# Each slot of the high and low weights 64 bytes longer than its chunk, and the low parts of x and h 32 bytes further on

## The reference

```python
for layer in range(DEPTH_2):
    g = norm_gains[layer]
    h = x + 0.5 * swiglu(rmsnorm_2(x, g[0]), w_ffn_gu[layer, 0], w_ffn_down[layer, 0])
    xn = rmsnorm_2(h, g[1])
    ...
    h = h + mix
    h = h + 0.5 * swiglu(rmsnorm_2(h, g[2]), w_ffn_gu[layer, 1], w_ffn_down[layer, 1])
    gate = jax.nn.sigmoid(rmsnorm_2(h, g[3]) @ w_ple_gate[layer])
    x = h + gate * (p[layer] @ w_ple_proj[layer])
```

## The kernel before

| distance in a partition, bytes | before |
|---|---|
| from `w_hi` to `w_lo`, same slot | 24960 |
| from one slot to the next | 4096 |
| from `w_lo` slot 0 to `xn_hi` | 24768 |
| from `xn_hi` to `xn_lo` | 16384 |
| from `xn_lo` to `h_hi`, then to `h_lo` | 16384, 4096 |

## Time and profile before

### The profile page before, as it was taken

The page is one execution under the profiler, slowest core; times in us unless marked ns, Lnnn a source line. Parts: engine busy times, 40 slices in busy tenths (PEclk is TensorE's granted clock), DMA queues, the critical chain, the costliest instruction groups (busy, mean ns, idle before and its releaser), DMA issues.

```text
span 2417.1 us, 51817 instructions
## 1 busy us (share of the span) xinstructions
PE 2405.2 (100%) x20462; PEld 2376.4 (98%) x20462; DVE 1725.2 (71%) x2425; ACT 1317.1 (54%) x2019; POOL 90.2 (4%) x91
## 2 busy tenths in 40 slices
PE   9999999999999999999999999999999999999999
PEld 9999999999999999999999999999999999999999
DVE  8878867558776677667766776688667766877666
ACT  5756655447564464445544554467445544766444
POOL 1000000001100000000000000000000000220000
PEclk9999999999999999999999999999999999999999
DMA  7325326555355556555466565643655656535653
GB/s 268 115 65 172 123 80 221 185 185 166 123 189 189 197 167 212 189 182 188 135 202 197 171 204 192 194 137 132 204 189 182 200 193 190 165 125 189 194 195 125
DMA packets 115378, 418.86 MB, mean 173 GB/s; under 512 B 12832, under 2 KB 14112, under 8 KB 114976
## 3 DMA queue, kind: packets, MB, share of 16 engines
q1 hardware_dynamic: 114096, 412.40, 52.2%
q0 software_dynamic: 560, 2.10, 0.3%
q10 hardware_dynamic: 576, 2.27, 0.2%
HBM read 414.62 MB, written 2.10 MB: 172 GB/s over the span
## 4 chain that ended last, share of the span: by engine, by line
PE 94%; DVE 3%; ACT 2%; DMA 1%; issue 0%; ACTq 0%; SPq 0%; DVEq 0%
PE ps_gu L140 17%; PE ps_gu L146 17%; PE ps_gu L141 17%; PE ps_acc L140 8%; PE ps_acc L146 8%; PE ps_acc L141 8%; PE ps_acc L2739 1%; PE ps_acc L2297 1%; DVE w_lo L100 1%; PE ps_misc L140 1%; PE ps_gu L2333 1%; PE ps_misc L141 1%; PE ps_misc L146 1%; PE ps_sum L140 1%; PE ps_sum L146 1%; PE ps_sum L141 1%
## 5 line engine op out<-in xcount | busy, mean ns | idle before, releaser
L100 DVE TENSOR_TENSOR w_lo<-w_raw,w_hi 128x1024 fp32r<-128x1024 f32 x781 | 953.0, 1228 | 378.8 <-ACT w_hi L92 370.3
L140 PE MATMUL ps_gu<-xn_hi,w_hi 128*128 128x256 f32 x3832 | 1055.7, 279 | 1.6 <-DVE w_lo L100 0.8
L141 PE MATMUL ps_gu<-xn_hi,w_lo 128*128 128x256 f32 x3832 | 1045.8, 277 | 0.0
L92 ACT ACTIVATE w_hi<-w_raw 128x1024 fp32r<-128x1024 f32 x781 | 819.4, 1056 | 360.9 <-PE ps_gu L146 264.3
L146 PE MATMUL ps_gu<-xn_lo,w_hi 128*128 128x256 f32 x3832 | 1010.1, 277 | 0.0
L140 PEld LDWEIGHTS ps_gu<-xn_hi,w_hi 128*128 128x128 f32 x3832 | 719.2, 188 | 4.5 <-issue 2.0
L141 PEld LDWEIGHTS ps_gu<-xn_hi,w_lo 128*128 128x128 f32 x3832 | 719.5, 188 | 0.3
L146 PEld LDWEIGHTS ps_gu<-xn_lo,w_hi 128*128 128x128 f32 x3832 | 696.8, 188 | 0.0
L140 PE MATMUL ps_acc<-h_hi,w_hi 128*128 128x256 f32 x1496 | 415.4, 278 | 0.0
L146 PE MATMUL ps_acc<-h_lo,w_hi 128*128 128x256 f32 x1496 | 413.6, 276 | 0.0
L141 PE MATMUL ps_acc<-h_hi,w_lo 128*128 128x256 f32 x1496 | 413.5, 276 | 0.0
(11 more groups left out here) (472 smaller groups left out, 2640.3 us busy)
## 6 DMA issues: line engine op xcount, KB each, us to landing
w_raw<-in_w_dram SPq DMA_DIRECT2D x781, 512.0 KB, 4.1
const<-in_const_dram SPq DMA_DIRECT2D x1, 1216.0 KB, 8.8
distance_rows<-arena POOLq DMA_DIRECT2D x1, 1024.0 KB, 6.9
p_all<-distance_rows POOLq DMA_DIRECT2D x2, 512.0 KB, 6.6
p_all<-in_p_dram ACTq DMA_DIRECT2D x1, 1024.0 KB, 6.5
out_dram<-x_res SPq DMA_DIRECT2D x8, 128.0 KB, 1.9
x_res<-in_x_dram SPq DMA_DIRECT2D x1, 512.0 KB, 5.9
x_res<-in_x_dram ACTq DMA_DIRECT2D x1, 512.0 KB, 7.3
```

What stands on the lines that cost most here:

```text
L92: act.activation(self.w_hi[:, s, :], self.w_raw[:, r, :], ACT.Copy).then_inc(self.w_hi_ready.sem, 1)
L100: dve.tensor_tensor(self.w_lo[:, s, :], self.w_raw[:, c % NR, :], self.w_hi[:, s, :], ALU.subtract)\
L140: pe.matmul(out, self.w_hi[:, s, j0:j0 + width], rhs_hi, start=start, stop=False, skip_group_check=True)
L141: pe.matmul(out, self.w_lo[:, s, j0:j0 + width], rhs_hi, start=False, stop=False, skip_group_check=True)
```

## The change

The slots of `w_hi` and `w_lo` become `CH + APART` = 1040 numbers long (4160 bytes), of which a chunk fills the first 1024. The tensor `low_apart` leaves its place between `w_hi` and `w_lo`, becomes 8 numbers (32 bytes) and stands between `xn_hi` and `xn_lo`. `x_apart`, between `w_lo` and `xn_hi`, becomes 80 numbers.

```diff
-LOW_APART, X_APART = 96, 48
+APART, LOW_APART, X_APART = 16, 8, 80
...
     k.w_raw = k.sb("w_raw", [P, NR, CH])
-    k.w_hi = k.sb("w_hi", [P, NS, CH], F32R)
-    k.sb("low_apart", [P, LOW_APART])
-    k.w_lo = k.sb("w_lo", [P, NS, CH], F32R)
+    k.w_hi, k.w_lo = (k.sb(name, [P, NS, CH + APART], F32R)[:, :, 0:CH] for name in ("w_hi", "w_lo"))
     k.sb("x_apart", [P, X_APART])
     k.xh = [k.sb(f"xn_hi{b}", [P, KD, S], F32R) for b in range(2)]
+    k.sb("low_apart", [P, LOW_APART])
     k.xl = [k.sb(f"xn_lo{b}", [P, KD, S], F32R) for b in range(2)]
     k.h_hi = k.sb("h_hi", [P, 4, S], F32R)
     k.h_lo = k.sb("h_lo", [P, 4, S], F32R)
```

## The result

The changed kernel took **2488.9 us** in the median of five runs (2486.21 to 2489.53). The kernel before, with two more runs beside it, took 2419.17 (2413.22 to 2420.61). The ratio is 1.0292, with an interval from 1.0275 to 1.0309: slower by 2.9%. The prediction had said 2410 and a range up to 2446. The profiled execution of the changed kernel has a span of 2487.5 us, 70.4 more than that of before.

What follows compares the result with a forecast made beforehand. TensorE's pace from matmul to matmul was taken as the bound. Slots -9.9 us, low parts 0, VectorE and ScalarE 0: 2420.2 - 9.9 = 2410.3, so 2410 us, range 2399 to 2446.

Steps and rivals of the forecast that it cites:

- What bounds the kernel: Whole kernel: TensorE's pace from one matmul to the next sets the end, 113.3 or 118.9 ns, not transfers or splits.
- Term 3: VectorE and ScalarE on the same slots: better places save at most 3 and 11 ns, hidden by idle time; 0.
- The sign that the distance matters: In the slow window L140 lasts 283 ns against 279 for L141; the three products differ only in where operands lie.
- The term of -9.9 us: Longer weight slots end the slow pace: 8.4 us in the first feed-forward block, 1.5 in four shorter stretches.
- Term 2: Low parts of x and h 32 bytes further on: new distances for the products reading them, taken as 0.
- the upper end that I named: Low parts' shift: at worst the slow pace for two products in three of gate or up chunks, more of down.
- the 86 us: Slots' worst bound: loss if all the remaining products took the slow pace, 15,400 x 5.6 ns.
- some slots slow TensorE down: Rival on the weight slots: each bad slot costs 11.8 us, giving 2422, 2434, 2446; two or more, chance 0.30.
- its dearest case: All six weight slots force the slow pace on TensorE: about 2500 us.
- Nothing changes: Rival: paces depend on how a run of products begins, not operand places; 2420 us, chance 0.18 with one bad slot.
- a faster pace than 113.3: Rival: some relation speeds all products by 1.8%, 37 us more gain, 2373 us; chance 0.08.
- the first term: The changed weight slots break the slow pace from chunk to chunk, saving 9.9 us.

Runs made afterwards that it cites:

- one odd slot: Against the kernel before, only slot 1 of w_hi and w_lo lies last and 64 bytes further on: 2485.55 us, ratio 1.028.
- 320/448/448: Weight tile start past moving operand start, bytes modulo 512, for w_lo beside xn_hi, w_hi beside xn_hi, w_hi beside xn_lo; the kernel before, 2419.17 us.
- 448/64/64: The same three distances once xn_hi and all behind it lie 128 bytes nearer than in the kernel before: 2408.45 us, ratio 0.9966.

## Why the prediction was wrong

**What bounds the kernel: right.** The pace of TensorE is the whole of it. The steps between products gave 68.6 of the 70.4 us. No wait appeared, and the splits stayed at 1227 and 1055 ns. Term 3, VectorE and ScalarE at 0, held.

**The sign that the distance matters: right.** The pace depends on the distance between the weight tile and the moving operand, leaving out multiples of 512 bytes. Moving both by 32 bytes, or one of them by 512, changes nothing (2416.32, 2414.58); moving one against the other by 32 or 64 gives 2479 to 2506.

**The step that failed is the first:** "A rhythm that lives on one relation then meets another after each chunk, after 24 matmuls. I take it that the slow pace no longer lasts from chunk to chunk." I applied this to the slow pace alone. The fast pace lives on one relation as well, and it is the one that broke. With one odd slot of six, the other five go at 2.853 us a chunk: the disturbance returns every six chunks, and in between the relation of before doesn't bring the fast pace back. The trace of before had shown this much: both paces last at the same relation, so there the slow one doesn't heal by itself. A change that breaks the rhythm at each chunk could only help if the slow pace were the fragile one. The term of -9.9 us came out as about +66 (slots alone, 2481.14 against 2414.74 for the runs beside it).

**Term 2, the low parts, was mis-sized:** taken as 0, and by itself +64 us (2479.09 against 2414.74). The choice of 0 leant on the earlier trace rows, a place with a small difference. But the earlier trace rows were matmuls of another width and without three different operand pairs, and the upper end that I named, the slow pace for two products in three, would have been two thirds of the 86 us, 57, and more for the down chunks. That end is what came. The two terms together give 74 us (2488.9 against the same 2414.74) rather than 131, since nearly every product is slow with either one.

**The rival "some slots slow TensorE down" was right in kind,** and its dearest case, all slots, "about 2500", is nearly what came. Its price was wrong: 12 us for the first bad slot, counted as if the others kept their pace. The run with one odd slot puts it at 72. So a price that grows by 12 us for each bad slot, 2422, 2434, 2446, doesn't hold, and the range ended on such a count. One bad slot was enough to slow the five that could be fast. Its count of 18,744 products, 24 for each chunk, is 300 over the 18,444 of the trace, which is under 2 us of its 86.

**"Nothing changes" and "a faster pace than 113.3" both fell.** By the Trainium skill, SBUF — State Buffer, section "Who interferes with whom", TensorE has two independent read ports and never waits on anyone. The prediction drew from it that places don't matter, and with that the runs disagree: with equal work, placement alone moves the kernel between 2408 and 2506 us. Who waits for whom within TensorE's two reads they don't show. And none of the windows shown, of any placement, holds more than 1326 matmuls in 150 us, so 113.3 ns is still the best seen.

**The gain that I looked for exists, by another way.** With x and h 128 bytes nearer the slow stretches of before all but vanish, and the span of the profiled execution falls by 11.0 us, from 2417.1 to 2406.1, where the first term said 9.9. Between the medians of the runs it is 6.2 us, since about half of the executions of before are some 7 us shorter anyway (below). All three runs that the prediction started from were of the longer kind, and its 5 us for what a measurement can tell was too small. Making all slots alike at a relation that heals did it. Making them different did not.

Left open: what in the memory or in TensorE makes the paces, and why h recovers at its old relation behind slow chunks of 2.80 us, while slots at that relation don't behind an odd slot. Most relations were not tried, nor was a stagger of 512 bytes, which would keep every relation.

## What to carry to other kernels

Where TensorE is the bound and never waits, count matmuls in windows of equal length before and after any change of layout: busy time and waits hide a loss of 5 ns each. When a trace shows two paces for equal work, ask which of them returns by itself after a disturbance before you disturb it; one odd slot is a cheap experiment for that, and here it cost 72 us at one relation and 16 at another. Treat the distance between the weight tile and the moving operand as a tuning parameter, keep it the same in every slot, and measure it again after anything is allocated in between.

## What the runs showed of the hardware that was not expected

- **Placement is worth up to 4%.** The same 18,444 products took 2408 to 2506 us over distances that differ by 32 to 128 bytes.
- **Two lasting paces at one placement.** At 320/448/448 a chunk takes 2.720 or 2.853 us, and the next ones keep to it until something disturbs them. At 448/64/64 the slow one ends within about five products.
- **The kernel before has two times.** Its 22 runs beside three of the kernels fall into 12 from 2411.1 to 2414.7 and 10 from 2419.3 to 2421.6, with nothing between. With everything 32 bytes on it is four from 2410.0 to 2414.0 and four from 2418.7 to 2420.9; with x and h 512 bytes on one of the eight lies between, at 2416.6. The profiled execution of before has the slow first block (1499) and a span of 2417.1; those of the two shifted kernels have it fast (1571, 1572) and spans of 2410.4 and 2407.9. I take that block for the difference, since 8.4 us is the price worked out for it and about 7 is the gap, but a fast execution of before itself was not profiled. With 448/64/64, eleven runs lie within 3.9 us, all of them under the shortest of the 22.
